# A decoder layer's paged attention: page loads in pairs with trailing rows and rope keys, and low parts moved between GpSimd and VectorE

## The chip, the cores and the metric

One core of one Trainium2 chip. The metric is the time of one execution on the device, in microseconds (us), as the median of several executions. A profiled execution has its own time and, inside it, the span from the first to the last instruction that the profiler recorded.

## The reference, cut to what matters

One decoder layer runs for 512 tokens of a new prompt and for 8 sequences of 8 new tokens each, which share all weights: a half-step of a SwiGLU feed-forward network, a combined projection, a convolution branch and an attention branch that are gated and merged, and a second half-step of a feed-forward network. The change touches only the attention of the 8 sequences over their cache:

```python
def one_seq(args):
    q_s, ckv_new, kpe_new, pages = args
    ckv = jnp.concatenate([cache_ckv_l[pages].reshape(past, KV_LORA), ckv_new], axis=0)
    kpe = jnp.concatenate([cache_kpe_l[pages].reshape(past, QK_ROPE), kpe_new], axis=0)
    k = build_keys(ckv, kpe, w_uk, k_head_norm)
    return attn_core(q_s, k, ckv, q_pos, k_pos, w_uv)
```

`past` is 2048 positions in 16 pages of 128. A page number comes from an int32 table and points into a pool. `build_keys` multiplies the 256 latent values of a position by `w_uk` (8 heads x 64), appends the 32 rope values and normalises each key by its root mean square; `attn_core` is 8 heads' softmax attention with the latents as values.

## The kernel before

**Precision.** Matmuls run on float32r operands split in two: `hi` is the rounded value (ScalarE copies it), `lo` the rest (a subtraction), and a product is hi x hi + hi x lo + lo x hi.

**The page stage.** `sequences` (L509) writes the loop over the 8 sequences: sequence 0 in straight code, then 1 to 4 in a hardware loop of two iterations of two, then 5, 6, 7 in straight code, on each compute engine. SyncE has a loop of its own (L778): sequences 0 and 1 are straight code, 2 to 7 a loop of three iterations of two. A sequence is 16 pages in 8 pairs. Three copies of a page are fetched, each by one transfer: transposed (`c_ring`, 128 KB, L731), as rows with the rope values beside them (`c_nat`, 144 KB, L737), and the rope keys transposed (`kpeT`, L742).
- *ScalarE* (`act_seq`, L1334): `pages_hi` (L1295) copies a pair of the ring into `cT_hi` (two slots); it needs the pair's transfers and TensorE done with the pair two before. For each page it copies scores from PSUM and squares the keys. In the same pass it makes `p_two` and the exponentials of the sequence before (`soft_act`) and the high parts of its rows (`pair_high`, L1328).
- *VectorE* (`dve_seq`, L2603): `pages_lo` (L2463) makes `cT_lo` of the next pair, 8 a sequence; the key sums (L2646); the softmax steps of the sequence before (`soft_dve`, L2497), the first of which (L2504) waits for GpSimd's squares; some taps of the convolution.
- *GpSimd* (`squares`, L950): for the sequence before, `split_pair` (L933), the low parts of row pairs 0 to 3, then `probabilities_low` (L941) in two halves, then row pairs 4 to 7; at the end it waits for this sequence's rows and squares their rope values (L962 to L964), for the key norms.
- *TensorE* (`pe_seq`, L1828): per page 12 products of 288 columns (L1861) that need `cT_lo` of the pair; after pages 3, 7, 11 and 15 one product with the rope keys of four pages (`kpe_scores`, L1818); at pages 12 and 15 the probabilities x values of the sequence before (L1781, L1782), each pair after `split_made`.

For sequence 7, the last, the sequence before (6) has its values multiplied without the split.

**The order of SyncE's queue.** SyncE issues everything in program order. `page_of` (L725) reads a page number from the table in SBUF into a register; it costs four instructions on the queue. `load_pages` (L744) goes by groups of four pages: four page numbers, a wait for the ring (`ct_lo`, both pairs two groups earlier), four ring transfers, a wait for `pe_scored`, four rope-key transfers with the same four registers, a wait for `pages_used`, four row transfers with the same registers. The ring has 8 slots (4 pairs), `kpeT` two groups, `c_nat` two sequences. L756 to L775 are the loads of sequence 0, woven into the waits of the stage before. Behind the loop come the first weights of the merge (`load_merge`, L611), which ScalarE splits in the midst of sequence 7 (L1367).

## Time and profile before

| | us |
|---|---|
| median of 3 runs | 1537.03 (1536.82 to 1539.36) |
| profiled execution, its own time | 1533.52 |
| its span, first to last instruction | 1531.5 |
| TensorE busy in the span | 1491.3 (97%) |
| VectorE / ScalarE / GpSimd busy | 1067.9 / 655.5 / 454.3 |
| page stage, first to last page product of TensorE | 706.8 to 1017.2 |
| `cT_lo` on VectorE | 64 of 0.69 (median) |
| `c_lo` on GpSimd | 48 of 1.20 (median) |

Busy times come from the profile's first part and from its groups of instructions; the start of an instruction is counted from the span's start. The profile doesn't count register, branch, semaphore and transfer-issuing instructions as busy, so SyncE has no busy time in it; its work is seen in the chain of waits (as "SPq") and in its timeline. TensorE's matmuls are pipelined and their ends are modelled, so its busy share is not its share of the peak. A busy time of 97% says little of a stage's limit: what counts is which wait ended last.

### The profile page before, as it was taken

Reading aid. Unit: us, or ns where it says so; the run is one execution under the profiler, and the core shown is the slowest. Engines: PE = TensorE matmul, PEld = TensorE weight load, DVE = VectorE, ACT = ScalarE, POOL = GpSimd, SP = SyncE. Lnnn points to the kernel's source line nnn. Section 1 sums busy time; section 2 is a strip of 40 time slices with the busy share of each in tenths; the row PEclk is TensorE's granted clock in tenths of the full one; section 3 lists DMA queues with packets and bytes.
Section 4 is the critical chain, followed back from the end, with each engine's and each line's share of the span. In section 5 each row is a group of like instructions: output and inputs, shape, how many; then the busy total and the mean of one; then the engine's idle time right before and its main releaser. Section 6 shows DMA issues by size and latency. Waiting matters only on the chain.

```text
span 1531.5 us, 31143 instructions
## 1 busy us (share of the span) xinstructions
PE 1491.3 (97%) x10771; PEld 1434.9 (94%) x10771; DVE 1067.9 (70%) x1738; ACT 655.5 (43%) x1215; POOL 454.3 (30%) x463
## 2 busy tenths in 40 slices
PE   8999999999999999999999888999999999999999
PEld 8999999999999999588888888888999999999999
DVE  7999898421269975865888788854759998985000
ACT  6444445322221242464666666642434444445111
POOL 4000002454465744320344333223551000005432
PEclk9999999999999999999999999999999999999999
DMA  6233234222333651003444443432222332332322
GB/s 176 70 103 103 82 97 116 78 83 75 82 83 100 83 116 47 13 4 99 129 127 129 124 125 111 128 106 72 83 83 56 109 97 85 106 92 81 91 77 82
DMA packets 245460, 141.69 MB, mean 93 GB/s; under 512 B 22705, under 2 KB 242290, under 8 KB 245362
## 3 DMA queue, kind: packets, MB, share of 16 engines
q1 hardware_dynamic: 244498, 139.97, 33.1%
q8 instruction: 54, 0.88, 0.2%
q10 hardware_dynamic: 864, 0.48, 0.1%
q14 instruction: 44, 0.36, 0.1%
HBM read 136.82 MB, written 3.58 MB: 92 GB/s over the span
## 4 chain that ended last, share of the span: by engine, by line
PE 52%; issue 24%; SPq 11%; POOL 7%; DVE 3%; ACT 1%; DMA 1%; POOLq 0%; DVEq 0%; ACTq 0%
PE ps L493 28%; PE ps L1522 14%; POOL w_lobuf L468 7%; SPq L726 3%; SPq L731 3%; SPq L742 3%; SPq L737 2%; PE ps L1861 2%; PE ps L1647 1%; PE ps L1701 1%; PE ps L1676 1%; PE ps L479 1%; PE ps L1691 1%; DMA w_rawbuf<-in_ffn_w_gu 1%; DVE cT_lo L2466 1%
## 5 line engine op out<-in xcount | busy, mean ns | idle before, releaser
L468 POOL TENSOR_TENSOR w_lobuf<-w_rawbuf,w_hibuf 128x256 fp32r<-128x256 f32 (+1 forms) x328 | 316.4, 996 | 801.4 <-ACT w_hibuf L461 801.3
L1522 PE MATMUL ps<-xs,w 128*128 128x288 f32 x3192 | 427.7, 296 | 0.8 <-DVE w L1984 0.8
L1522 PEld LDWEIGHTS ps<-xs,w 128*128 128x128 f32 x3192 | 426.8, 188 | 1.5 <-issue 1.5
L461 ACT ACTIVATE w_hibuf<-w_rawbuf 128x1024 fp32r<-128x1024 f32 (+1 forms) x89 | 104.4, 1173 | 353.3 <-PE ps L493 332.9
L2192 DVE SCALAR_TENSOR_TENSOR xT<-ps,xT 128x576 f32<-128x576 f32 x23 | 17.4, 756 | 202.4 <-PE ps L493 202.4
L1984 DVE TENSOR_TENSOR w<-w_raw,w 128x512 fp32r<-128x512 f32 x228 | 154.0, 690 | 0.3 <-ACT w L1029 0.2
L493 PE MATMUL ps<-a_hi,w_lobuf 128*128 128x288 f32 x682 | 147.5, 297 | 0.0
L493 PE MATMUL ps<-a_hi,w_hibuf 128*128 128x288 f32 x682 | 147.2, 296 | 0.0
L493 PE MATMUL ps<-x_hi,w_hibuf 128*128 128x288 f32 x656 | 142.2, 298 | 4.1 <-POOL w_lobuf L468 2.9
L493 PE MATMUL ps<-a_lo,w_hibuf 128*128 128x288 f32 x682 | 145.5, 294 | 0.0
L493 PE MATMUL ps<-x_lo,w_hibuf 128*128 128x288 f32 x656 | 140.8, 296 | 0.0
L493 PE MATMUL ps<-x_hi,w_lobuf 128*128 128x288 f32 x656 | 140.7, 296 | 0.0
L1029 ACT ACTIVATE w<-w_raw 128x512 fp32r<-128x512 f32 x228 | 132.2, 624 | 5.7 <-DVE w_raw L1978 2.4
L1861 PE MATMUL ps<-kq_hi,cT_hi 128*128 128x288 f32 x512 | 119.6, 316 | 14.7 <-DVE cT_lo L2466 9.3
L2215 DVE SCALAR_TENSOR_TENSOR y<-ext,cols,y 128x512 f32<-128x512 f32 x120 | 110.6, 922 | 4.1 <-DVE y L2215 1.4
L1861 PE MATMUL ps<-kq_hi,cT_lo 128*128 128x288 f32 x512 | 111.3, 299 | 0.0
L1861 PE MATMUL ps<-kq_lo,cT_hi 128*128 128x288 f32 x512 | 111.3, 299 | 0.0
L493 PEld LDWEIGHTS ps<-x_hi,w_hibuf 128*128 128x128 f32 x656 | 105.4, 188 | 5.8 <-POOL w_lobuf L468 4.1
L493 PEld LDWEIGHTS ps<-a_hi,w_hibuf 128*128 128x128 f32 x682 | 110.2, 189 | 0.0
L493 PEld LDWEIGHTS ps<-a_lo,w_hibuf 128*128 128x128 f32 x682 | 109.3, 188 | 0.0
L493 PEld LDWEIGHTS ps<-a_hi,w_lobuf 128*128 128x128 f32 x682 | 109.0, 188 | 0.0
L1861 PEld LDWEIGHTS ps<-kq_hi,cT_hi 128*128 128x128 f32 x512 | 84.1, 194 | 25.3 <-DVE cT_lo L2466 10.4
(335 smaller groups left out, 2602.6 us busy)
## 6 DMA issues: line engine op xcount, KB each, us to landing
w_raw<-in_ffn_w_gu SPq DMA_DIRECT2D x76, 256.0 KB, 2.9
up_rows<-in_ffn_w_gu SPq DMA_DIRECT2D x72, 256.0 KB, 3.2
c_nat<-in_pages_in SPq DMA_DIRECT2D x128, 144.0 KB, 2.2
c_ring<-in_pages_t SPq DMA_DIRECT2D x128, 128.0 KB, 2.1
w_rawbuf<-in_w_in SPq DMA_DIRECT2D x58, 256.0 KB, 3.2
w_rawbuf<-in_ffn_w_down SPq DMA_DIRECT2D x32, 384.0 KB, 4.0
w_rawbuf<-in_ffn_w_down SPq DMA_DIRECT2D x32, 320.0 KB, 3.4
w_rawbuf<-in_ffn_w_gu SPq DMA_DIRECT2D x24, 256.0 KB, 3.4
```

What stands on the lines that cost most here:

```text
L461: act.activation(w_hibuf[:, r % HIS, 0:size], w_rawbuf[:, r, 0:size], ACT.Copy).then_inc(w_hi_done, 1)
L468: ins = pool.tensor_tensor(w_lobuf[:, r, part], w_rawbuf[:, r, part], w_hibuf[:, r % HIS, part].bitcast(F32), ALU.subtract)
L493: mm = pe.matmul(ps[0:width, 2 * s + h, 0:HALF], a, b[:, k, h * HALF:(h + 1) * HALF], start=first and i == 0 and j == 0, stop=last and i = ...
L726: return sp.value_load(pages[0:1, ds(s * NP + t, 1)], min_val=0, max_val=pages_t.shape[0] - 1)
L731: sp.dma_start(c_ring[:, (4 * g + u + RING // 2) % RING, :], pages_t[ds(page, 1), :, :].rearrange("a p c -> (a p) c"))\
L737: sp.dma_start(c_nat[:, b, 4 * g + u, :], pages_in[ds(page, 1), :, :].rearrange("a p c -> (a p) c")).then_inc(nat_in[b][g], 16)
L742: sp.dma_start(kpeT[u * DR:(u + 1) * DR, g % 2, :], pages_k[ds(page, 1), :, :].rearrange("a d t -> (a d) t")).then_inc(kpe_in[g % 2], 16)
L1029: act.activation(w7[b][:, slot, 0, :], src, ACT.Copy).then_inc(w7_hi, 1)
L1522: mm = pe.matmul(ps[:, seven_bank(f, slot), 0:HALF], m, xs[:, slot, n, k, :], start=k == 0 and j == 0, stop=k == KH - 1 and j == 2)
L1861: mm = pe.matmul(ps[:, page_banks(t) + half, 0:KQ], a, m[:, half, cols], start=k == 0 and j == 0, stop=k == 1 and j == 2)
L1984: dve.tensor_tensor(w7[b][:, slot, 1, :], w7_raw[b][:, slot, 1, :], w7[b][:, slot, 0, :].bitcast(F32), ALU.subtract).then_inc(w7_lo, 1)
L2215: dve.scalar_tensor_tensor(dst, src, cw, dst, op0=ALU.mult, op1=ALU.add).then_inc(conv_p_step, 1)
```

## The change

- **The ring** is refilled pair by pair: each pair has its own semaphore and waits for the low part of the pair four before.
- **The rows trail**: row pairs 0 to 3 of a sequence are fetched with its ring pairs 4 to 7, row pairs 4 to 7 with the next sequence's ring pairs 0 to 3 (behind the loop for the last one). `nat_in` becomes one semaphore for a buffer, so who reads rows waits for all 16 pages.
- **The rope keys trail**: group 0 is fetched with ring pair 3, group 1 with 5, group 2 with 7, group 3 with pair 1 of the next sequence.
- **Page numbers** are read by `found` where each of the three is issued: two for a ring pair, two for a row pair, four for a group of rope keys.
- **Pages' low parts** (`pages_lo`) move from VectorE to GpSimd, but for sequence 0's. GpSimd does one a pair, with the row pairs' low parts at pairs 2, 3, 6 and 7; the low part of the next sequence's pair 0 comes ahead of the wait for the rows and the squares.
- **Probabilities' low parts** move from GpSimd to VectorE, at pair 5, with a semaphore `p_low` that TensorE waits for once a sequence.

```diff
--- before.py
+++ after.py
@@ -323,8 +323,8 @@
         prep_q, prep_tr, prep_copied, prep_mm, prep_lat, ready_new, uk_split = (sem(n) for n in (
             "prep_q", "prep_tr", "prep_copied", "prep_mm", "prep_lat", "ready_new", "uk_split"))
         ukT_done = sem("ukT_done")
-        nat_in = [[sem(f"nat_in{b}{g}") for g in range(NP // 4)] for b in range(2)]
-        ring_in = [sem(f"ring_in{g}") for g in range(2)]
+        nat_in = [sem(f"nat_in{b}") for b in range(2)]
+        ring_in = [sem(f"ring_in{j}") for j in range(RING // 2)]
         kpe_in = [sem(f"kpe_in{g}") for g in range(2)]
 
         def ring_pair(pp):
@@ -519,7 +519,7 @@
         PAIRS, EARLY_PAIRS = NP // 2, len(c_hi)
-        SPLITS = PAIRS + 2
+        SPLITS = PAIRS
@@ -533,7 +533,7 @@
 
         def pair_made(r, j):
 
-            return r * SPLITS + (EARLY_PAIRS + 1 if j < EARLY_PAIRS else j + 3)
+            return r * SPLITS + (j + 1)
 
         def high_made(r, j):
 
@@ -546,6 +546,12 @@
             return STACKED * HIGHS + (r - STACKED) * 2 + (1 + half)
 
         PEB = 6
+
+        def pages_lo(eng, s, pp):
+
+            eng.wait_ge(ct_hi, s * PAIRS + (pp + 1))
+            eng.tensor_tensor(cT_lo[:, pp % 2, :], ring_pair(pp), cT_hi[:, pp % 2, :].bitcast(F32), ALU.subtract).then_inc(ct_lo, 1)
+
 
         LN_MEAN, LN_VAR = (NS - 3, 8), (NS - 2, 10)
         THIRD = T // 3
@@ -725,59 +731,78 @@
             def page_of(s, t):
                 return sp.value_load(pages[0:1, ds(s * NP + t, 1)], min_val=0, max_val=pages_t.shape[0] - 1)
 
...
+            def found(s, t0, n):
+                return [page_of(s, t0 + u) for u in range(n)]
+
+            def load_ring(pp, two):
+
+                for u, page in enumerate(two):
+                    sp.dma_start(c_ring[:, (2 * pp + u + RING // 2) % RING, :], pages_t[ds(page, 1), :, :].rearrange("a p c -> (a p) c"))\
+                        .then_inc(ring_in[pp % (RING // 2)], 16)
+
+            def load_rows(b, pp, two):
+
+                for u, page in enumerate(two):
+                    sp.dma_start(c_nat[:, b, 2 * pp + u, :], pages_in[ds(page, 1), :, :].rearrange("a p c -> (a p) c")).then_inc(nat_in[b], 16)
+
+            def load_kpe(s, g):
+
+                four = found(s, 4 * g, 4)
+                if not (isinstance(s, int) and s == 0 and g < 2):
                     sp.wait_ge(pe_scored, s * (NP // 4) + (g - 1))
+                for u, page in enumerate(four):
+                    sp.dma_start(kpeT[u * DR:(u + 1) * DR, g % 2, :], pages_k[ds(page, 1), :, :].rearrange("a d t -> (a d) t"))\
+                        .then_inc(kpe_in[g % 2], 16)
+
+            def load_pair(s, b, pp, used=None):
+
+                two = found(s, 2 * pp, 2)
+                sp.wait_ge(ct_lo, s * PAIRS + (pp - 3))
+                load_ring(pp, two)
+                if pp >= PAIRS // 2:
+                    q = pp - PAIRS // 2
+                    two = found(s, 2 * q, 2)
                     if used is not None:
+                        sp.wait_ge(pages_used, used + (q + 1))
+                    load_rows(b, q, two)
+                elif used is not None:
+                    q = pp + PAIRS // 2
+                    two = found(s - 1, 2 * q, 2)
+                    sp.wait_ge(pages_used, used + (q + 1 - PAIRS))
+                    load_rows(1 - b, q, two)
+                if pp % 2:
+                    load_kpe(s - 1 if pp == 1 else s, 3 if pp == 1 else (pp - 3) // 2)
 
             sp.wait_ge(rows_done, 2 * NT + PT_TILES)
+            for pp in range(2):
+                load_ring(pp, found(0, 2 * pp, 2))
+            load_kpe(0, 0)
             sp.wait_ge(prep_q, 1)
+            for pp in range(6):
+                load_rows(0, pp, found(0, 2 * pp, 2))
             sp.wait_ge(prep_tr, 2)
             sp.wait_ge(uk_split, 1)
+            for pp in range(2, 4):
+                load_ring(pp, found(0, 2 * pp, 2))
+            load_kpe(0, 1)
+            for pp in range(6, PAIRS):
+                load_rows(0, pp, found(0, 2 * pp, 2))
+            for pp in range(4, PAIRS):
+                two = found(0, 2 * pp, 2)
+                sp.wait_ge(ct_lo, pp - 3)
+                load_ring(pp, two)
+            load_kpe(0, 2)
             sp.wait_ge(prep_mm, 2)
+            for pp in range(PAIRS):
+                load_pair(1, 1, pp)
             with sp.Fori(1, NS // 2) as i:
                 for b in range(2):
+                    for pp in range(PAIRS):
+                        load_pair(i * 2 + b, b, pp, i * (2 * PAIRS) + (EARLY_PAIRS + PAIRS * (b - 2)))
+            for q in range(PAIRS // 2, PAIRS):
+                sp.wait_ge(pages_used, EARLY_PAIRS + PAIRS * (NS - 3) + (q + 1))
+                load_rows(1, q, found(NS - 1, 2 * q, 2))
+            load_kpe(NS - 1, 3)
 
             sp.wait_ge(lat_mm, STACKED)
             for t in range(2):
@@ -938,28 +963,22 @@
                                    c_hi[j % EARLY_PAIRS][:, :, 0:KL].bitcast(F32), ALU.subtract)\
                     .then_inc(split_made, 1)
 
-            def probabilities_low(r, b, half):
-
-                t = slice(half * NP // 2, (half + 1) * NP // 2)
-                pool.wait_ge(p_done, exp_made(r, half))
-                ins = pool.tensor_tensor(p_two[:, t, 1, :], s_buf[:, b, t, :], p_two[:, t, 0, :].bitcast(F32), ALU.subtract)
-                if half:
-                    ins = pool.tensor_tensor(p_two[0:TS, NP, 1, :], s_buf[0:TS, b, NP, :], p_two[0:TS, NP, 0, :].bitcast(F32), ALU.subtract)
-                ins.then_inc(split_made, 1)
-
             def squares(s, b, uses, prev, nxt):
 
-                if prev and stacked(s):
-                    for j in range(EARLY_PAIRS):
-                        split_pair(s - 1, 1 - b, j)
-                    for half in range(2):
-                        probabilities_low(s - 1, 1 - b, half)
-                    for j in range(EARLY_PAIRS, PAIRS):
-                        split_pair(s - 1, 1 - b, j)
+                later = not (isinstance(s, int) and s == 0)
+                for pp in range(PAIRS):
+                    if later and pp < PAIRS - 1:
+                        pages_lo(pool, s, pp + 1)
+                    if prev and stacked(s):
+                        for j in ((), (), (0, 1), (2, 3), (), (), (4, 5), (6, 7))[pp]:
+                            split_pair(s - 1, 1 - b, j)
+                if not later:
+                    pool.wait_ge(ct_lo, PAIRS)
+                if nxt:
+                    pages_lo(pool, s, PAIRS)
                 if not nxt:
                     split_lo(pool, n_merge, n_merge % RAWS, KD * P)
-                for g in range(NP // 4):
-                    pool.wait_ge(nat_in[b][g], uses * 64)
+                pool.wait_ge(nat_in[b], uses * (16 * NP))
                 k = c_nat[:, b, :, KL:KL + DR]
                 pool.tensor_tensor(k, k, k, ALU.mult).then_inc(kpe_sq, 1)
 
@@ -1294,7 +1313,7 @@
 
             def pages_hi(s, pp):
 
-                act.wait_ge(ring_in[pp // 2 % 2], (s * 2 + (pp // 4 + 1)) * 64)
+                act.wait_ge(ring_in[pp % (RING // 2)], (s * 2 + (pp // 4 + 1)) * 32)
                 if not (isinstance(s, int) and s == 0 and pp < 2):
                     act.wait_ge(page_mm, s * NP + (2 * pp - 2))
                 act.activation(cT_hi[:, pp % 2, :], ring_pair(pp), ACT.Copy).then_inc(ct_hi, 1)
@@ -1327,7 +1346,7 @@
 
             def pair_high(r, b, j, uses):
 
-                act.wait_ge(nat_in[b][j // 2], uses * 64)
+                act.wait_ge(nat_in[b], uses * (16 * NP))
                 act.wait_ge(pages_used, r * PAIRS + (j + 1))
                 act.activation(c_hi[j % EARLY_PAIRS][:, :, 0:KL], c_nat[:, b, 2 * j:2 * j + 2, 0:KL], ACT.Copy).then_inc(p_done, 1)
 
@@ -1773,6 +1792,7 @@
                 pe.matmul(ps[:, 7, 0:HQ], ones[0:HQ, :], diag[:, :], start=True, stop=True).then_inc(max_mm, 1)
                 yield
                 if stacked(r + 1):
+                    pe.wait_ge(p_low, r + 1)
                     for j in range(PAIRS):
                         pe.wait_ge(split_made, pair_made(r, j))
                         for u in range(2):
@@ -2600,12 +2615,22 @@
 
                 tap(CT - 1, k, k + AT_LOOP if not isinstance(k, int) or k else None)
 
+            def probabilities_low(r, b):
+
+                for half in range(2):
+                    t = slice(half * NP // 2, (half + 1) * NP // 2)
+                    dve.wait_ge(p_done, exp_made(r, half))
+                    dve.tensor_tensor(p_two[:, t, 1, :], s_buf[:, b, t, :], p_two[:, t, 0, :].bitcast(F32), ALU.subtract)
+                dve.tensor_tensor(p_two[0:TS, NP, 1, :], s_buf[0:TS, b, NP, :], p_two[0:TS, NP, 0, :].bitcast(F32), ALU.subtract).then_inc(p_low, 1)
+
             def dve_seq(s, b, uses, prev, nxt):
                 soft = soft_dve(s - 1, 1 - b) if prev else None
                 taps = iter(range(PER))
                 for pp in range(NP // 2):
-                    if pp + 1 < NP // 2 or nxt:
-                        pages_lo(s, pp + 1)
+                    if isinstance(s, int) and s == 0 and pp + 1 < PAIRS:
+                        pages_lo(dve, s, pp + 1)
+                    if prev and stacked(s) and pp == 5:
+                        probabilities_low(s - 1, 1 - b)
                     if prev and pp < (5 if stacked(s) else 6):
                         next(soft)
                     if pp == 4 and nxt:
```

## Rows read from the trace of the kernel before

**Rows 1.** The page, part 4: the chain that ended last, by engine.
```profile
PE 52%; issue 24%; SPq 11%; POOL 7%; DVE 3%; ACT 1%; DMA 1%; POOLq 0%; DVEq 0%; ACTq 0%
```

**Rows 2.** The same chain from 768 to 996 us: shares by line; longest piece (start, us).
```profile
by line: issue 23.0%; SPq L726 15.4%; SPq L731 14.4%; SPq L737 14.0%; SPq L742 13.5%; DVE cT_lo L2466 2.9%; DVE page_ss L2646 2.4%; PE ps L1861 2.2%; DVE ln_acc L2579 1.0%; ACT cT_hi L1300 1.0%; DMA c_ring<-in_pages_t 0.9%; DVE mx L2520 0.9
...
839.74 2.65 issue
```

**Rows 3.** Timeline of SyncE in the loop: start us, us, engine, line, operation, count.
```profile
824.41 1.90 SPq L731 DMA_DIRECT2D c_ring<-in_pages_t  x4
826.56 1.84 SPq L742 DMA_DIRECT2D kpeT<-in_pages_k  x4
828.64 1.92 SPq L737 DMA_DIRECT2D c_nat<-in_pages_in  x4
833.41 1.89 SPq L731 DMA_DIRECT2D c_ring<-in_pages_t  x4
...
837.64 1.92 SPq L737 DMA_DIRECT2D c_nat<-in_pages_in  x4
845.27 0.87 SPq L731 DMA_DIRECT2D c_ring<-in_pages_t  x2
```

**Rows 4.** Timeline of SyncE in sequence 1 (straight code) and its last burst.
```profile
736.96 1.92 SPq L737 DMA_DIRECT2D c_nat<-in_pages_in  x4
741.29 1.88 SPq L731 DMA_DIRECT2D c_ring<-in_pages_t  x4
...
763.33 1.91 SPq L737 DMA_DIRECT2D c_nat<-in_pages_in  x4
```

**Rows 5.** Line 726, page numbers: duration ns min/median/max, first and last start us.
```profile
L726 SPq TENSOR_LOAD <-pages x140: 260/265/477, 644.7 to 988.0; - x140
```

**Rows 6.** SyncE's waits, 645 to 1020 us: total, times, longest.
```profile
SPq L737 <- DVE rope_rep L2441: 37.5, 1, 37.5
...
SPq L742 <- PE ps L1825: 3.0, 2, 2.5
```

**Rows 7.** Windows: us, busy PE, PEld, DVE, ACT, POOL (instructions), PEclk, DMA share, GB/s.
```profile
862.00:899.00 37.00, 33.73 (x244) 31.87 (x243) 32.81 (x53) 24.98 (x60) 15.07 (x12) 1.00 0.44 130
...
1007.00:1014.00 7.00, 6.44 (x30) 6.19 (x30) 5.27 (x9) 2.98 (x8) 3.31 (x4) 0.56 0.25 75
```

**Rows 8.** Line 1861's idle time by its end (us, times); ScalarE's waits, 744 to 1018.
```profile
  DVE cT_lo L2466: 19.7, 27
...
ACT cT_hi L1300 <- DMA c_ring<-in_pages_t: 13.3, 9, 3.5
```

**Rows 9.** Low parts by line (ns), and the timelines of VectorE and GpSimd where two meet.
```profile
L937 POOL TENSOR_TENSOR c_lo<-c_nat,c_hi x48: 1187/1200/1732, 747.2 to 966.0; 128x512 fp32r<-128x512 f32 x48
L2466 DVE TENSOR_TENSOR cT_lo<-c_ring,cT_hi x64: 627/692/1523, 706.0 to 1010.0; 128x512 fp32r<-128x512 f32 x64
L945 POOL TENSOR_TENSOR p_two<-s_buf,p_two x12: 1270/1279/1285, 760.8 to 957.9; 128x512 fp32r<-128x512 f32 x12
L947 POOL TENSOR_TENSOR p_two<-s_buf,p_two x6: 768/774/866, 763.9 to 959.1; 64x64 fp32r<-64x64 f32 x6
...
784.84 5.66 POOL L937 TENSOR_TENSOR c_lo<-c_nat,c_hi 128x512 fp32r<-128x512 f32 x4 [11.09 <-ACT c_hi L1332]
786.95 1.31 DVE L2466 TENSOR_TENSOR cT_lo<-c_ring,cT_hi 128x512 fp32r<-128x512 f32 x1
```

**Rows 10.** Timelines of SyncE, ScalarE and TensorE at the end of the stage.
```profile
992.96 2.69 SPq L737 DMA_DIRECT2D c_nat<-in_pages_in  x4
...
1001.21 1.06 ACT L461 ACTIVATE w_hibuf<-w_rawbuf 128x1024 fp32r<-128x1024 f32 x1 [6.06 <-DMA w_rawbuf<-in_w_conv_out]
1004.35 0.61 ACT L1300 ACTIVATE cT_hi<-c_ring 128x512 fp32r<-128x512 f32 x1
1007.56 0.37 PE L1808 MATMUL ps<-ones,den_sum 128*64 128x1 f32 x2 [3.11 <-DVE den_sum L2540]
1017.70 0.53 PE L493 MATMUL ps<-y_hi,w_hibuf 128*128 128x288 f32 x2
```

More of the change, by code:

```diff
@@ L726, in page_of @@
                 return sp.value_load(pages[0:1, ds(s * NP + t, 1)], min_val=0, max_val=pages_t.shape[0] - 1)
-            def load_ring(g, found):
-                for u, page in enumerate(found):
-                    sp.dma_start(c_ring[:, (4 * g + u + RING // 2) % RING, :], pages_t[ds(page, 1), :, :].rearrange("a p c -> (a p) c"))\
-                        .then_inc(ring_in[g % 2], 16)
-            def load_rows(b, g, found):
-                for u, page in enumerate(found):
-                    sp.dma_start(c_nat[:, b, 4 * g + u, :], pages_in[ds(page, 1), :, :].rearrange("a p c -> (a p) c")).then_inc(nat_in[b][g], 16)
@@ L739, in load_kpe @@
-            def load_kpe(g, found):
-                for u, page in enumerate(found):
-                    sp.dma_start(kpeT[u * DR:(u + 1) * DR, g % 2, :], pages_k[ds(page, 1), :, :].rearrange("a d t -> (a d) t")).then_inc(kpe_in[g % 2], 16)
-            def load_pages(s, b, used=None):
-                for g in range(NP // 4):
-                    found = [page_of(s, 4 * g + u) for u in range(4)]
-                    sp.wait_ge(ct_lo, s * PAIRS + (2 * g - 2))
-                    load_ring(g, found)
-                    sp.wait_ge(pe_scored, s * (NP // 4) + (g - 1))
-                    load_kpe(g, found)
-                    if used is not None:
-                        sp.wait_ge(pages_used, used + 2 * (g + 1))
-                    load_rows(b, g, found)
+            def found(s, t0, n):
+                return [page_of(s, t0 + u) for u in range(n)]
@@ L756, in _ @@
             sp.wait_ge(rows_done, 2 * NT + PT_TILES)
-            found = [page_of(0, u) for u in range(4)]
-            load_ring(0, found)
-            load_kpe(0, found)
+            for pp in range(2):
+                load_ring(pp, found(0, 2 * pp, 2))
+            load_kpe(0, 0)
             sp.wait_ge(prep_q, 1)
-            load_rows(0, 0, found)
-            for g in (1, 2):
-                load_rows(0, g, [page_of(0, 4 * g + u) for u in range(4)])
+            for pp in range(6):
+                load_rows(0, pp, found(0, 2 * pp, 2))
@@ L764, in _ @@
             sp.wait_ge(prep_tr, 2)
             sp.wait_ge(uk_split, 1)
-            found = [page_of(0, 4 + u) for u in range(4)]
-            load_ring(1, found)
-            load_kpe(1, found)
-            load_rows(0, 3, [page_of(0, 12 + u) for u in range(4)])
-            for g in (2, 3):
-                found = [page_of(0, 4 * g + u) for u in range(4)]
-                sp.wait_ge(ct_lo, 2 * g - 2)
-                load_ring(g, found)
-                sp.wait_ge(pe_scored, g - 1)
-                load_kpe(g, found)
+            for pp in range(2, 4):
+                load_ring(pp, found(0, 2 * pp, 2))
@@ L2461, in _ @@
             ins.then_inc(uk_split, 1)
-            def pages_lo(s, pp):
-                dve.wait_ge(ct_hi, s * PAIRS + (pp + 1))
-                dve.tensor_tensor(cT_lo[:, pp % 2, :], ring_pair(pp), cT_hi[:, pp % 2, :].bitcast(F32), ALU.subtract).then_inc(ct_lo, 1)
             dve.wait_ge(prep_tr, 3)
@@ L2483, in queries_lo @@
                 ins.then_inc(q_split, 1)
-            pages_lo(0, 0)
+            pages_lo(dve, 0, 0)
             dve.wait_ge(prep_lat, 2)
```

5 lines of the change are left out of this document (1 added, 4 removed).

## The prediction

> **What bounds the kernel now.** I began with the page's chain of what ended last [rows 1]: TensorE holds 52% of it, but SyncE's queue holds 11% and "issue" (time in which an engine waited for nothing that the profile shows) 24%. Work that only issues transfers has no place in the chain unless something waits for it, so the next view was the same chain cut to the loop over the cached pages, 768 to 996 us [rows 2]. There the four SyncE lines hold 15.4 + 14.4 + 14.0 + 13.5 = 57% and "issue" 23%; TensorE's page products (L1861) hold 2.2%. Its longest piece is 2.65 us of issue at 839.74: SyncE's branch back to the top of its loop. So in this stage the queue that fetches pages sets the pace.
>
> SyncE's own timeline says why [rows 3]. A group of four pages is three bursts: 4 transposed pages in 1.90 us, 4 rope keys in 1.84, 4 row pages in 1.92. A transfer starts every 0.52 us ((1.90 - 0.33)/3; the last one's issue is 0.33). From the end of the row burst (830.56) to the next ring transfer (833.41) lie 2.85 us, and in them are the four page-number loads of L726, which run one after another on the same queue. Less the 0.19 us that any transfer needs ahead of its issue (0.52 - 0.33), that is 0.66 us a load. In straight code the gap is 741.29 - 738.88 = 2.41 us, so 0.555 us a load [rows 4]. One loop sequence is then 48 x 0.52 + 16 x 0.66 = 35.5 us plus half of a back edge (the 839.56 to 845.27 gap is 5.7 us instead of 2.85), 37.0 us. The six loop sequences took 995.65 - 765.24 = 230.4 us [rows 4, 10], 38.4 us each.
>
> Does the queue ever rest? Between 645 and 1020 us it waited on semaphores among the sequences' page loads for 3.0 us (L742, twice); the 37.5 us at L737 lie before the sequences begin [rows 6]. There is no slack to put more into. TensorE, in contrast, has some: 33.7 us busy in a 37 us sequence [rows 7], and the waits that the change aims at are small: 19.7 us for the pages' low parts and 13.3 us of ScalarE for ring pages, over all eight sequences [rows 8].
>
> **The change part by part.**
>
> *Page-number loads.* Does a load happen once per page, or once per call? The trace of before has 140 of them [rows 5]. The code calls page_of 28 times for sequence 0 (twelve of these pages a second time), 16 for sequence 1 and 16 for each of six more: 140. So repeated ones are not shared. After the change the ring, the rows and the rope keys look up their pages separately: one load per page transfer. Transfers are three a page, 3 x 128 = 384, so loads are 384, 244 more. Where they fall:
> - Before the sequences: 20 instead of 12. These 8 are covered by the 37.5 us wait [rows 6]: nothing. Without it, they would cost 4.4 us.
> - Straight code from the second ring pair to the end of sequence 1, and behind the loop: 24 + 40 + 12 = 76 instead of 32, 44 more at 0.555 = 24.4 us.
> - The loop, six sequences: 48 instead of 16, 192 more at 0.66 = 126.7 us.
>
> *Waits.* A sequence has 20 places where SyncE checks a semaphore, instead of 12. In the loop each costs an address step of about 0.06 us: from the end of the ring burst to the key burst are 0.25 us (826.31 to 826.56), 0.19 of them the transfer's own. 48 x 0.06 = 2.9 us. The transfers are the same in number and size, so their issue costs nothing more.
>
> *What was slack.* The 3.0 us that SyncE waited before are swallowed: -3.0. The finer ring waits (pair p for the low part of pair p-4) are met well ahead when the queue paces everything: the low part it asks for needs only ScalarE's copy of a page pair that TensorE had two pairs earlier. That is also so across the trailing transfers. Group g's rope keys now come with ring pair 2g+3, so TensorE stops at pages 3, 7, 11 and 15 for them; but no ring wait needs TensorE further than that. The rows' last pairs come in the next sequence's first half, and GpSimd (L962) and VectorE (L2504) stand still for them; what they hold back is pair 1's low part, which SyncE asks for only four slots later (pair 5). I price these waits at nothing because the queue's 58 us a sequence cover them; if that cover were gone they would be the next thing (rival C).
>
> *Low parts on GpSimd.* 56 of the 64 move: 1.20 us there instead of 0.69 on VectorE (the 1.20 us is the same shape in L937) [rows 9], 56 x 0.51 = 29 us more of engine time, and nothing on the path. GpSimd's per-sequence load is 15.1 us [rows 7]; with eight lows instead of the probabilities' (2 x 1.28 + 0.77 us) it becomes about 21 of 58. The probabilities' low parts on VectorE replace lows of 8 x 0.69 us by about 2 us: it gains time that it doesn't need. Here a row bears on a risk: VectorE's low part at 786.95 took 1.31 us while GpSimd ran its own subtraction from 784.84 [rows 9]. More such overlaps could add up to 8 x 0.62 = 5 us a sequence to VectorE, which was busy 32.8 us of 37 [rows 7]; that too fits into 58. The Trainium skill, "SBUF — State Buffer", section "Who interferes with whom", has it that a VectorE instruction with two SBUF inputs contends with a GpSimd one that reads SBUF, and the loser blocks; by that rule the move speaks against itself, and the trace agrees (1.31 against 0.69 us).
>
> *Back edge and stalls.* A sequence grows from 220 to 356 instructions (four a load, three a transfer, one a wait). Of the 230.4 us of the six, 6 x 36.2 (with the waits' steps) + 5.7 for two back edges explain 223; 7 us are stretched issues. If they grow with the length they add 4 us, if not 0: I take 2.
>
> *The end of the stage.* From the last page transfer (995.65) to the first product of the merge (1017.70) are 22.0 us [rows 10]: the weight transfer right behind it, the ScalarE split that waits for it at 1001.21, then the high part of the next pair at 1004.35, then TensorE. That chain keeps its order, since the last rope keys are again issued just ahead of those weights. It becomes about 1.5 us longer (VectorE's sum of the probabilities now follows the page sums that ScalarE was late with). After it nothing changes.
>
> Sum: 24.4 + 126.7 + 2.9 - 3.0 + 2 + 1.5 = 154.5 us. The profiled execution took 1533.5 us (span 1531.5), 3.5 below the median of the runs, 1537.0. So 1688.0 against its own time, and 1691.5, say 1692, as a median.
>
> **The rivals.**
>
> *A, the forecast (0.84).* SyncE needs 48 x 0.52 + 48 x 0.66 + 20 x 0.06 = 57.8 us a sequence and everything else waits.
>
> *B, the stalls go and the loads are free (0.03), faster.* If a page-number load could run beside the transfers, the queue would again need 37 us, and the change would take away TensorE's 19.7 us for low parts and some of the ring waits: about 25 us, 1512. It turns at 25/236 = 0.1 us a load. Against it: the measured gaps of 2.85 and 2.41 us, in which nothing else is on the queue. The Trainium skill speaks for it, in "DMA: Bandwidth & Descriptors", section "Issuing engines are not separate DMA queues": the sequencer's time to initiate a DMA is usually small relative to the DMA. By that rule the queue isn't the bound; the trace disagrees, for the 48 issues of a sequence alone take 25 of its 37 us and leave the queue, with the loads, no rest.
>
> *C, loads at half price (0.04).* If only the load itself (0.265 us, [rows 5]) stayed and the register steps around it overlapped, 236 x 0.265 = 63 us; the queue then needs 39 us plus the new key and row waits of TensorE, GpSimd and VectorE: about 1600.
>
> *D, TensorE turns cold and becomes a second bound (0.09), slower still.* It now stands still four times a sequence for 4 to 8 us. After the 3.1 us wait ahead of 1007.56 [rows 10] the granted clock was 0.56 over 1007 to 1014 [rows 7]. At the lower level, 1.2 GHz, throughout, its 32 us of work would be 64, above 58: seven sequences x 6 = 42 us more, 1734. Against it: the rows show full clock again within the 7 us that follow, and four times 2 to 3 us fit into 58. It decides if the clock stays down for more than half of the work.
>
> **How the numbers follow.** Likeliest A, 1692. Its bounds: all loads at 0.555 us, 236 x 0.555 = 131 us instead of 151 and no stall growth give 1670; back edges that cost double (6 us), all stalls in proportion (2 more) and some cold TensorE time at the end of the stage (3) give 1704. Reaching towards D and for what I could not see of the instruction supply of a longer loop, the range is 1664 to 1722. About 0.2% is what a measurement of this kernel can tell from no change. Faster by more than that 0.03 (B), within it 0.01, slower 0.96.
>
> **What would show it.** In the changed kernel's profile: 384 loads at page_of; SyncE's sequences about 58 us long, with bursts of two transfers and 1.3 us between them; no wait of SyncE on ct_lo; in the loop's chain SyncE and "issue" above 85%; TensorE idle at the rope-key products and VectorE and GpSimd waiting for c_nat; TensorE below 60% busy between 780 and 1140 us, with a granted clock clearly below 1; the stage ending near 1174 instead of 1018; everything behind it shifted as a block. Wrong would be: fewer loads, a load below 0.4 us, or SyncE waiting on ct_lo or pe_scored for more than 10 us, which would put TensorE or the low parts in charge.

## The result and the profile after

The changed kernel takes 1666.74 us (median of 4 runs, 1665.25 to 1669.21) and the kernel before, in the same comparison, 1536.92 (1534.81 to 1539.36): a ratio of 1.0846 [1.0825, 1.0867], slower by 129.8 us. The forecast was 1692, in a range of 1664 to 1722. Direction, mechanism and range hold; the size was 25 us too large. In the profiled executions the span grew from 1531.5 to 1664.2 us, +132.7 where the sum had +154.5. One run of this document, an execution of E3 with 1794.27 us at a granted clock of 0.751, was in a slow state and is left out of E3's numbers below.

The page of the changed kernel: span, busy times, TensorE and its granted clock in 40 slices, and the chain by engine.

```profile
span 1664.2 us, 31938 instructions
PE 1530.0 (92%) x10771; PEld 1473.6 (89%) x10771; DVE 1048.8 (63%) x1700; ACT 657.0 (39%) x1215; POOL 505.5 (30%) x501
PE   8999999999999999997577776867999999999999
PEclk9999999999999999998887788878999999999999
PE 49%; issue 26%; SPq 14%; POOL 8%; DMA 1%; ACT 1%; DVE 1%; POOLq 0%; ACTq 0%
```

SyncE's queue now holds 14% of the chain, and "issue" 26%, against 11 and 24 [rows 1]. TensorE was at work nearly all the time except in slices 19 to 28, the stage with the cached pages; its clock falls in the same slices. The chain cut to that stage (780 to 1110 us), by line, with one of its longest pieces:

```profile
by line: SPq L732 32.8%; issue 30.3%; SPq L746 10.2%; SPq L740 10.1%; SPq L754 9.4%; POOL c_lo L962 2.2%; POOL cT_lo L553 1.9%; PE ps L1881 1.5%; PE ps L1801 0.6%; PE ps L1802 0.6%; DMA kpeT<-in_pages_k 0.6%; SPq L760 0.4%; PE ps L1845 0.4%
...
887.78 2.68 issue
```

The reading of page numbers, now L732, goes from 15.4% [rows 2] to 32.8%, while the three transfer lines fall from 14 or so to 10 each. With "issue" the four lines make up 92.8%. Not all of this "issue" is the queue's: up to 818 us the chain runs through GpSimd, with idle pieces of 13.32 us (at 787.25) and 5.55 (774.52). From 820 to 1110 us, where it runs through the queue, the same view reads

```profile
by line: SPq L732 37.2%; issue 24.0%; SPq L746 11.6%; SPq L740 11.2%; SPq L754 10.7%; PE ps L1881 1.7%; PE ps L1801 0.7%; PE ps L1802 0.7%; DMA kpeT<-in_pages_k 0.6%; SPq L760 0.4%; PE ps L1845 0.4%; SPq L766 0.2%; SPq L771 0.2%; SPq L752 0
```

which is 94.7% with its 24.0% of "issue". The count of the reads, over the whole kernel (duration ns min/median/max, first and last start us):

```profile
L732 SPq TENSOR_LOAD <-pages x384: 260/267/479, 645.1 to 1128.6; - x192
```

384 instead of 140 [rows 5], and one of them takes what it took. SyncE's timeline in the loop (start, us, engine, line, operation, count), to be laid beside [rows 3]:

```profile
857.78 1.84 SPq L754 DMA_DIRECT2D kpeT<-in_pages_k  x4
861.21 1.21 SPq L740 DMA_DIRECT2D c_ring<-in_pages_t  x2
863.82 0.87 SPq L746 DMA_DIRECT2D c_nat<-in_pages_in  x2
866.26 0.86 SPq L740 DMA_DIRECT2D c_ring<-in_pages_t  x2
868.49 0.86 SPq L746 DMA_DIRECT2D c_nat<-in_pages_in  x2
871.75 1.86 SPq L754 DMA_DIRECT2D kpeT<-in_pages_k  x4
875.18 0.90 SPq L740 DMA_DIRECT2D c_ring<-in_pages_t  x2
```

A burst of two takes 0.86 us, and 1.4 to 1.6 us pass before the next one (2.4 before the four keys): the queue spends more time on finding pages than on asking for them. SyncE's waits on semaphores, 645 to 1160 us (total, times, longest), and the waits of the others for rows, keys and low parts (longer ones, up to GpSimd's 185.8 us for ScalarE's copies, are of engines that wait for each other):

```profile
SPq L732 <- DVE rope_rep L2461: 35.7, 1, 35.7
SPq L811 <- POOL cT_lo L553: 10.8, 1, 10.8
SPq L776 <- PE ps L1677: 6.7, 1, 6.7
```
```profile
POOL c_nat L983 <- DMA c_nat<-in_pages_in: 82.2, 6, 15.8
PE ps L1845 <- DMA kpeT<-in_pages_k: 60.5, 20, 6.1
PE ps L1881 <- POOL cT_lo L553: 57.6, 8, 10.0
DVE kpe_ss L2520 <- POOL c_nat L983: 55.3, 6, 10.2
```

The first of these waits lies ahead of the sequences, as before [rows 6], and so does the one at L776 (`rows_done`); L811, and two of 5 us at the merge's weights (L624, L621), stand in the code behind the page loads. So none is at the page loads of the sequences. TensorE, GpSimd and VectorE stand still for the trailing keys and rows, as the prediction had it, and for low parts whose pages came late. They wait beside each other and all for the queue, so their sum means nothing.

### The profile page after: what moved, and what is told of

Read it like the earlier page. It is cut to its first block, busy times and chain, and to the rows that moved or that the text cites. A ratio compares the mean times of both kernels' runs of the same rounds, so it can differ in the third digit from the quotient of the medians.

```text
span 1664.2 us, 31938 instructions
## 1 busy us (share of the span) xinstructions
PE 1530.0 (92%) x10771; PEld 1473.6 (89%) x10771; DVE 1048.8 (63%) x1700; ACT 657.0 (39%) x1215; POOL 505.5 (30%) x501
## 4 chain that ended last, share of the span: by engine, by line
PE 49%; issue 26%; SPq 14%; POOL 8%; DMA 1%; ACT 1%; DVE 1%; POOLq 0%; ACTq 0%
PE ps L493 26%; PE ps L1541 13%; SPq L732 7%; POOL w_lobuf L468 6%; SPq L746 2%; PE ps L1881 2%; SPq L740 2%; SPq L754 2%; PE ps L1666 1%; PE ps L1720 1%; PE ps L1695 1%; POOL cT_lo L553 1%; PE ps L1822 1%; POOL c_lo L962 1%; DMA w_rawbuf<-in_ffn_w_gu 1%
## 5 line engine op out<-in xcount | busy, mean ns | idle before, releaser
L1881 PE MATMUL ps<-kq_hi,cT_hi 128*128 128x288 f32 x512 | 131.5, 341 | 59.4 <-POOL cT_lo L553 57.6
L1881 PEld LDWEIGHTS ps<-kq_hi,cT_hi 128*128 128x128 f32 x512 | 94.9, 216 | 66.4 <-POOL cT_lo L553 36.0
L2671 DVE TENSOR_REDUCE page_ss<-sq 128x8 f32<-128x512 f32 x128 | 84.2, 677 | 99.9 <-ACT sq L1370 99.8
L553 POOL TENSOR_TENSOR cT_lo<-c_ring,cT_hi 128x512 fp32r<-128x512 f32 x56 | 77.4, 1382 | 185.8 <-ACT cT_hi L1319 185.8
L1881 PE MATMUL ps<-kq_hi,cT_lo 128*128 128x288 f32 x512 | 120.2, 319 | 0.0
L1881 PE MATMUL ps<-kq_lo,cT_hi 128*128 128x288 f32 x512 | 118.7, 316 | 0.0
```

Of the source, the lines that this page charges most:

```text
L553: eng.tensor_tensor(cT_lo[:, pp % 2, :], ring_pair(pp), cT_hi[:, pp % 2, :].bitcast(F32), ALU.subtract).then_inc(ct_lo, 1)
L1881: mm = pe.matmul(ps[:, page_banks(t) + half, 0:KQ], a, m[:, half, cols], start=k == 0 and j == 0, stop=k == 1 and j == 2)
L2671: dve.tensor_reduce(page_ss[:, t, :], sq[:, u, 0:H * DN].rearrange("p (h d) -> p h d", d=DN), AX, ALU.add).then_inc(page_red, 1)
```

## The experiments

All ten kernels were timed against the kernel before, in three groups, each on one chip but every group on another; the medians of before in them were 1535.25 (E1 to E4), 1534.35 (E5 to E8) and 1535.9 us (E9, E10). Two theories stood at the start: the loss is the number of page-number reads (each holds SyncE's queue for about 0.55 us), or it is the trailing order and the new waits that starve TensorE.

### E1 and E10: the kernel before, with more reads and nothing else

```diff
                     load_kpe(g, found)
+                    found = [page_of(s, 4 * g + u) for u in range(4)]
                     if used is not None:
```

E10 has this line; E1 has it and the same one ahead of the wait for `pe_scored`. They apply to sequences 1 to 7: 112 and 224 reads more.

> The kernel before with one thing added: in sequences 1 to 7 SyncE reads the four page numbers of a group three times, ahead of the ring, of the rope keys and of the rows. 224 more loads, nothing else moved, no trailing transfers. The queue theory (SyncE's queue paces the page stage and a load runs alone on it): in the changed kernel a load without its own address step takes 0.56 us, so 224 x 0.56 = 125 us less the 3 us of slack, 1659 us (1650 to 1672), nearly all of the change's own loss. Rival (the loss comes from the waits that the trailing rows and rope keys put on TensorE, GpSimd and VectorE): the loads are mostly hidden, below 1560.

> The kernel before with the page numbers of each group read twice in sequences 1 to 7 (112 more loads, half of e1). If the queue is the bound throughout, the price a load is the same as in e1, 0.55 us: 112 x 0.55 = 62 us less at most 3 us of slack, 1595 us (1590 to 1600). Rival (the first loads are partly hidden, a knee between): below 1585.

Measured: E1 1659.29 us, ratio 1.0801 [1.0779, 1.0823], +124.0. E10 1594.65, ratio 1.039 [1.0375, 1.0404], +58.8. The reads in E1 and the chain from 768 to 1100 us:

```profile
L726 SPq TENSOR_LOAD <-pages x364: 260/267/479, 645.7 to 1115.8; - x182
```
```profile
by line: SPq L726 37.6%; issue 25.1%; SPq L737 12.4%; SPq L731 11.5%; SPq L742 10.8%; DMA c_ring<-in_pages_t 0.6%; PE ps L1783 0.5%; PE ps L1784 0.4%; DVE cT_lo L2468 0.2%; SPq L748 0.2%; SPq L755 0.2%; ACT cT_hi L1302 0.2%; SPq L751 0.2%; 
```

E1 costs 124.0 / 224 = 0.554 us a read and E10 58.8 / 112 = 0.525; with the 3.0 us of slack that both swallow, 0.567 and 0.552. The second 112 reads cost 65.2 us, the first 58.8, and of this difference of 6.4 us the slack makes 3.0, and the rest is within the two intervals (3.4 us either way for E1, 2.2 for E10): so the price is linear as far as these runs can tell, and there is next to no slack to be filled first. E1 keeps the order, the waits and the engines of before, and loses nearly all that the change loses: reads alone suffice.

### E2: the change, without its additional reads

```diff
-                four = found(s, 4 * g, 4)
+                four = found(s, 4 * g, 4) if four is None else four
...
                 two = found(s, 2 * pp, 2)
+                four, last[0] = (last[0] or []) + two, two
...
                     q = pp - PAIRS // 2
-                    two = found(s, 2 * q, 2)
...
                     q = pp + PAIRS // 2
-                    two = found(s - 1, 2 * q, 2)
```

The trailing rows and keys take the ring pairs' page numbers that are at hand. It leaves out that those transfers fetch the right pages; their number, size, places and waits are those of the change. 168 reads are left.

> The changed kernel with the page numbers of the ring pair used again for the row pair and the rope keys that are issued beside it, in sequences 1 to 7: 216 loads fewer, every transfer of the same size at the same place of the queue, every wait kept. It leaves out fetching the right pages for the trailing rows and rope keys. Queue theory: 216 x 0.57 = 123 us come back, 1544 us (1535 to 1556). Rival (trailing waits): it stays above 1620.

Measured: 1549.24 us, ratio 1.0085 [1.0064, 1.0106], +14.0. Trailing order, pairwise waits and moved low parts are all there, and 116 us of the loss are gone, 0.54 for each of the 216 reads. What is left is near 20 reads x 0.55 + 48 waits x 0.06 = 13.9 us (28 reads more than before, 8 of them under the wait ahead of the sequences). The rival theory falls.

### E3 and E4: pairs without trailing; the low parts alone

```diff
             def load_pair(s, b, pp, used=None):
                 two = found(s, 2 * pp, 2)
                 sp.wait_ge(ct_lo, s * PAIRS + (pp - 3))
                 load_ring(pp, two)
-                if pp >= PAIRS // 2:
...
+                if pp % 2:
+                    load_kpe(s, pp // 2, last[0] + two)
+                last[0] = two
+                if used is not None:
+                    sp.wait_ge(pages_used, used + (pp + 1))
+                load_rows(b, pp, two)
```

E3 (against the changed kernel, above) refills pair by pair and moves the low parts, but rows and keys follow their own ring pairs and share the numbers: 160 reads. E4 has SyncE's code of before, and of the change only GpSimd's `pages_lo` and VectorE's `probabilities_low`.

> The changed kernel with rows and rope keys no longer trailing in sequences 1 to 7: per pair two page numbers, the ring pair, at odd pairs four rope keys, then the row pair, all with the same page numbers. 16 loads a sequence as before, but refilled by pairs, with the low parts moved as in the change. Queue theory: the queue is as long as before but for 8 more waits a sequence (0.06 us each, 3 us in all), so 1535 us (1526 to 1545); the difference to e2 is what the trailing itself costs or brings. Rival (fine ring waits and the moved low parts bring the speed that was meant): below 1520.

> The kernel before with only the low parts moved: pages' low parts on GpSimd, probabilities' low parts on VectorE, SyncE's queue untouched. Queue theory: the queue covers it, 1537 us (1530 to 1543). Rival (GpSimd's 1.2 to 1.4 us a low part, and its meeting VectorE's two-input subtractions, are on the path): 56 x 0.5 = 28 us more, about 1560.

Measured: E3 1544.34 us, 1.0058 [1.0038, 1.0078], +9.1, where 12 x 0.55 + 2.9 is 9.5: the 1535 us expected (1526 to 1545) had left out 12 more reads in sequence 0's loads. The speed that was meant did not come. E4 1537.55, 1.0004 [0.999, 1.0017], no difference. SyncE's only wait at the page loads of sequences 1 to 7 in E4, and what TensorE waited for most at its page products, 705 to 1030 us:

```profile
SPq L748 <- PE ps L1827: 2.1, 1, 2.1
```
```profile
PE ps L1863 <- POOL cT_lo L553: 14.0, 10, 2.7
```

Moving the low parts to an engine that takes twice as long for one costs nothing and brings nothing here. That the queue decides when the pages come would be the reason, and E8 below, where they cost 3.4 us, fits it.

### E5 to E8: one instruction for several page numbers

Reads at 0.55 us on a full queue suggest the opposite edit: fewer of them. One load can fill several registers.

```diff
+            def many(s, t0, n):
+                return list(nc.values_load_multi_w_load_instructions(pages[0:1, ds(s * NP + t0, n)], engines=[mybir.EngineType.SP],
+                                                                     min_val=0, max_val=pages_t.shape[0] - 1,
+                                                                     skip_runtime_bounds_check_because="page numbers come from the table")[1])
...
-                    found = [page_of(s, 4 * g + u) for u in range(4)]
+                    found = many(s, 4 * g, 4)
```

It also leaves out the range check of each number. E5 is the kernel before with it, E8 is E4 with it, E6 is E3 with one for each pair, and E7 is the whole change with it in `load_pair` and `load_kpe`.

> The kernel before with one edit: in sequences 1 to 7 the four page numbers of a group come by one load instruction that fills four registers, without the range check of each number. The queue shrinks from 37 us a sequence to about 25.0 + 4 x 0.4 + 1 = 28 us. Queue theory: the queue really is the bound of the kernel before, so it gets faster until the next bound, TensorE's 32.5 us of work and its 4 us of waits a sequence: 37 instead of 38.4 us in the loop and 5 us in sequence 1, so about 1522 us (1512 to 1531). Rival (the queue was only just not in the way, TensorE's own chain sets the pace before): 1535 us, no change.

> e3 (pairs, not trailing, low parts moved) with one load instruction for the two page numbers of a pair: the queue is 25 + 8 x 0.4 + 1.2 = 29.5 us. If the fine ring waits and the moved low parts are worth anything, it shows here, where the queue is out of the way: 8 to 12 us below e5, about 1512. If they are worth nothing, equal to e5; if GpSimd's 1.2 us a low part is now on the path, 5 to 15 us above it.

> The whole change, trailing rows and rope keys too, right pages everywhere, with one load instruction wherever page numbers are read in sequences 1 to 7 (20 a sequence instead of 48). The queue is 25 + 20 x 0.42 + 1.2 = 34.6 us a sequence. Queue theory: all of the change's loss goes: 1525 to 1540. Rival (trailing waits): with the queue out of the way the waits for the trailing rows and keys remain, above 1560.

> e4 (the kernel before with the low parts moved) with e5's single loads. Against e5 it tells what the moved low parts are worth when the queue covers nothing: theory of the change, VectorE's lateness (19.7 us of TensorE's waits) goes, 10 us below e5; rival (GpSimd slower and in program order with the row pairs' low parts), 5 to 15 us above e5.

| kernel | median us | ratio to before [95%] |
|---|---|---|
| E5, before | 1526.49 | 0.9945 [0.9929, 0.9961] |
| E8, low parts moved | 1529.88 | 0.9971 [0.9959, 0.9982] |
| E6, and pair by pair | 1531.13 | 0.9975 [0.9966, 0.9985] |
| E7, and trailing (the change) | 1541.38 | 1.0043 [1.0027, 1.0058] |

In E5 the loads, SyncE's timeline, its waits from 705 to 1030 us, and the chain from 768 to 990:

```profile
L729 SPq TENSOR_LOAD <-pages x28: 295/299/317, 733.2 to 983.0; - x28
```
```profile
826.52 1.92 SPq L742 DMA_DIRECT2D c_nat<-in_pages_in  x4
829.14 1.88 SPq L736 DMA_DIRECT2D c_ring<-in_pages_t  x4
```
```profile
SPq L747 <- PE ps L1830: 60.2, 21, 7.2
```
```profile
by line: issue 20.9%; DVE page_ss L2651 12.8%; PE ps L1866 12.1%; DVE cT_lo L2471 11.9%; DVE mx L2525 3.6%; ACT sq L1356 3.4%; ACT cT_hi L1305 3.1%; DVE s_buf L2520 2.8%; DVE y L2220 2.6%; ACT s_buf L1327 2.6%; DVE s_buf L2659 2.0%; ACT p_t
```

The gap between rows and ring is 829.14 - 828.44 = 0.70 us instead of 2.85 [rows 3], and in sequence 1 it is 0.52 instead of 2.41 [rows 4]. 24 groups x 2.15 and 4 x 1.89, 59 us, are freed on the queue, and only 7.9 reach the end: SyncE now waits 60.2 us for the page scores at L747, and no SyncE line is left among the lines that the chain shows. The bound has passed to the engines. E5 beats both kernels and is the best version found; its gain is within the expected range but smaller than its value, since TensorE and VectorE were closer behind the queue than I had thought.

The ladder below it prices the change's other parts where the queue is no longer full. The low parts on GpSimd cost 1529.88 - 1526.49 = 3.4 us, with intervals that just touch. Pair by pair adds 1.2, which is nothing that these runs can tell, and it holds more on the queue: 12 plain reads in sequence 0 and eight loads a sequence of two numbers instead of four loads of four. Neither theory's value came: E8 was to be 10 us below E5 or 5 to 15 above, E6 8 to 12 below, equal, or 5 to 15 above, and it is 4.6 above. Trailing adds 10.2, but with it the queue gets more reads, and E7 ends just above the 1525 to 1540 that were expected. In E7 the loads are (whole kernel), with the chain from 768 to 990 us:

```profile
L735 SPq TENSOR_LOAD <-pages x140: 303/473/488, 650.6 to 1004.3; - x140
```
```profile
by line: issue 26.5%; SPq L735 20.7%; SPq L759 14.9%; SPq L745 14.9%; SPq L751 14.8%; PE ps L1886 3.0%; POOL cT_lo L553 1.9%; POOL c_lo L967 1.8%; SPq L765 0.6%; POOL c_nat L988 0.5%; SPq L776 0.3%; SPq L771 0.3%; SPq L757 0.2%; PE ps L1850
```

With 20 loads a sequence, most at 0.47 us, the queue is still the bound. So E7 doesn't tell what trailing is worth by itself. The loads of E6, all of two numbers, say which of them take 0.47:

```profile
L735 SPq TENSOR_LOAD <-pages x56: 462/476/497, 736.6 to 988.0; - x56
```

A load of two numbers takes 0.47 us here, in E9 and in E7 (108 of its 140, the other 32 being of four), and one of four 0.30 in E5, E8 and E7. The expectations had 0.4 for both.

### E9: trailing with a short queue

E9 is E2 with `many(s, 2 * pp, 2)` for the ring pairs: 8 loads a sequence and the change's order of transfers. Like E2 it leaves out that the trailing transfers fetch the right pages.

> e2 (the change with the ring pair's page numbers used again for the trailing rows and rope keys; the right pages of those are left out) with one load instruction a pair: 8 in a sequence, the same queue as e6, 29.5 us. The only difference to e6 is that rows and rope keys trail. If trailing costs nothing of its own: within 3 us of e6 once the 12 page numbers and transfers behind the loop are counted (12 x 1.07 = 13 us of queue ahead of the merge's weights, of which the short queue should cover a part), 1531 to 1540. Rival (trailing has its own price: GpSimd and VectorE wait for the last rows, TensorE for the keys): 1545 or more.

Measured: 1537.81 us, ratio 1.0012 [1.0, 1.0024]. By the ratios that is 0.0037 x 1535 = 5.7 us above E6, give or take 2.4 by the two intervals (E6 ran on another chip, so the times themselves aren't compared), and inside the expected 1531 to 1540. The longest wait of SyncE at page loads, in E9 first and then in E6, and the end of SyncE's page loads in the same order:

```profile
SPq L745 <- POOL cT_lo L553: 39.8, 28, 2.9
```
```profile
SPq L751 <- PE ps L1799: 16.4, 5, 4.6
```
```profile
984.69 1.85 SPq L759 DMA_DIRECT2D kpeT<-in_pages_k  x4
988.40 7.91 SPq L751 DMA_DIRECT2D c_nat<-in_pages_in  x8
998.73 1.85 SPq L759 DMA_DIRECT2D kpeT<-in_pages_k  x4
1000.68 0.41 SPq L624 DMA_DIRECT2D w_rawbuf<-in_w_conv_out  x1
```
```profile
994.63 0.40 SPq L624 DMA_DIRECT2D w_rawbuf<-in_w_conv_out  x1
```

In E9 the queue rests: it waits 39.8 us for the low parts that free its ring. Its page loads in the loop end at 986.54, but 12 reads and 12 transfers stand behind the loop, ahead of the merge's weights, which go out at 1000.68 instead of 994.63. These 6.05 us, of one execution each, agree with the 5.7: with a queue that has room, what trailing costs is accounted for by its tail. Even there it gains nothing over E6.

## Why the prediction was right, and where it was off

**What bounds the kernel**, right. The queue read off the gap of 2.85 us was the bound; E1 and E10 show it, without any other edit. It was so by less than the prediction made of it, and one reading of [rows 2] was wrong: the chain's longest piece from 768 to 996 us was not the 2.65 us at 839.74, but

```profile
917.24 3.06 issue
...
933.69 3.18 PE ps L1861 x24
```

From 925 to 972 us that chain runs through the transfers, ScalarE, VectorE and TensorE, so these were close behind the queue, as E5's gain of only 7.9 us shows too. The Trainium skill, "DMA: Bandwidth & Descriptors", section "Issuing engines are not separate DMA queues", says that the sequencer's time to initiate a DMA is usually small relative to the DMA. By the profile an issue took 0.52 us [rows 3] and a page's transfer 2.1 to 2.2 from issue to landing, so each one is the smaller part; but the issues run one after another. The runs disagree with the rule for this stage: what stands on the issuing queue set the time in E1, E10 and the change.

**244 more reads, 8 of them covered**, right: 384 in the trace, and no cost of the eight shows. But only four of them lie ahead of the 37.5 us wait; the other four were covered by one of 3.3 us in before (L765, for VectorE's `kq_lo`), which the prediction didn't name. The next ring burst started at 705.10 us instead of 705.76.

**0.66 us a read in the loop**, the step that failed: "The loop, six sequences: 48 instead of 16, 192 more at 0.66 = 126.7 us." The timeline above has it by kind of burst, each gap less the 0.19 us that a transfer needs ahead of its issue and the 0.06 of a wait's step. Ring pair, rows at 864.69 to ring at 866.26: (1.57 - 0.25)/2 = 0.66. Rows, ring at 867.12 to rows at 868.49: (1.37 - 0.25)/2 = 0.56. Keys, 869.35 to 871.75: (2.40 - 0.25)/4 = 0.54. The register steps of L726 before and L732 after, within the loop, go with it:

```profile
L726 SPq FUSED_REGOPS  x182: 46/152/164, 774.7 to 988.3; - x182
L726 SPq TENSOR_LOAD <-pages x92: 262/265/287, 774.8 to 988.0; - x92
```
```profile
L732 SPq FUSED_REGOPS  x402: 46/152/160, 777.1 to 1115.7; - x134
L732 SPq TENSOR_LOAD <-pages x286: 262/267/291, 777.2 to 1115.4; - x143
```

Before, two register steps a read: the check of about 0.15 us, and one of about 0.05. Now 1.4. That the short one is the address, and is shared by reads whose address is at hand, is an inference from the counts. The measured part is the price: most of the added reads are of the cheap kind. 192 x 0.55 is 105.6 instead of 126.7 us, 21 less, and that is nearly the whole error of 22. The lower price was in the range as a bound (1670), by the straight code's row; I took the price of the loop's own row, which held reads of the dearer kind alone. With it the law is short: 236 x 0.55 = 130 us, measured 129.8. That this comes out to the last digit is luck: waits and slack cancel, and so nearly do the two terms that follow.

**Waits 2.9, slack -3.0**, right as far as E2, E3 and E10 can tell.

**Back edges and stalls 2 us**, too small. The last page transfer ended at 995.65 before [rows 10] and at 1131.16 now, +135.5. The corrected terms give 24.4 + 105.6 + 2.9 - 3.0 = 129.9, so 5.6 are left for back edges and stretched issues, 4.6 of them in the loop; had the stalls grown in proportion it would have been 4. What they consist of wasn't resolved. The loop's body didn't grow as counted: by the trace SyncE ran some 216 and then 326 instructions a sequence, not 220 and 356, since an added read needs one register step and not two.

**End of the stage +1.5**, wrong in sign. From the last page transfer to the merge's first product it was 22.05 us and is now 1149.13 - 1131.16 = 17.97:

```profile
1129.32 1.84 SPq L754 DMA_DIRECT2D kpeT<-in_pages_k  x4
```
```profile
1134.87 1.06 ACT L461 ACTIVATE w_hibuf<-w_rawbuf 128x1024 fp32r<-128x1024 f32 x1 [21.66 <-DMA w_rawbuf<-in_w_conv_out]
...
1138.01 0.61 ACT L1319 ACTIVATE cT_hi<-c_ring 128x512 fp32r<-128x512 f32 x1
```
```profile
1129.55 0.28 PE L1828 MATMUL ps<-ones,den_sum 128*64 128x1 f32 x2
1149.13 0.53 PE L493 MATMUL ps<-y_hi,w_hibuf 128*128 128x288 f32 x2
```

ScalarE's split starts 3.71 us behind the last page transfer instead of 5.56 [rows 10]. TensorE's sum of the probabilities (L1828) starts at 1129.55, while everything waits for the queue; in before it came at 1007.56, behind that split and a wait of 3.11 us [rows 10]. I had argued only with the order of that chain, not with what the engines finish while they stand still. 135.5 - 4.1 and 1.3 us behind the stage make the 132.7 of the span.

**Work priced at nothing** stayed covered, as predicted: no page load of SyncE waits at L740, L746 or L754. The cover was the long queue. E5, E8 and E9 show what comes out without it: 3.4 us for the low parts, 6 for the tail, and SyncE waiting for TensorE or the low parts. The low parts on GpSimd took (ns min/median/max)

```profile
L553 POOL TENSOR_TENSOR cT_lo<-c_ring,cT_hi x56: 1257/1286/2342, 739.2 to 1142.9; 128x512 fp32r<-128x512 f32 x56
L553 DVE TENSOR_TENSOR cT_lo<-c_ring,cT_hi x8: 675/682/774, 707.7 to 735.9; 128x512 fp32r<-128x512 f32 x8
```

1.29 us instead of the 1.20 taken from another line [rows 9], and up to 2.34. One of these beside VectorE:

```profile
805.36 2.33 POOL L553 TENSOR_TENSOR cT_lo<-c_ring,cT_hi 128x512 fp32r<-128x512 f32 x1 [2.48 <-ACT cT_hi L1319]
```
```profile
805.32 1.21 DVE L2530 TENSOR_TENSOR s_buf<-s_buf,k_inv 128x1024 f32<-128x1024 f32 x1
```

The Trainium skill, "SBUF — State Buffer", section "Who interferes with whom", has a VectorE instruction with two SBUF inputs contend with a GpSimd one that reads SBUF, and one of them block; this pair agrees with it (the 2.33 us are 1.04 more than the usual 1.29, and VectorE's instruction ran beside it for 1.17), and E4 shows that it had no price here.

**The rivals.** B (free reads, 1512) and C (half price, 1600) fall: a read costs 0.55 us in E1. D's first half happened, its second not. TensorE's windows (us, busy PE, PEld, DVE, ACT, POOL, PEclk, DMA share, GB/s):

```profile
892.00:948.00 56.00, 38.83 (x234) 37.19 (x232) 26.95 (x44) 24.43 (x58) 21.89 (x17) 0.80 0.30 85
...
780.00:1140.00 360.00, 248.75 (x1491) 232.55 (x1489) 174.62 (x272) 152.95 (x359) 126.27 (x98) 0.83 0.30 85
```

The granted clock was 0.83 over the stage: part of it at the 1.2 GHz level after TensorE's pauses (behind its wait of 10.00 us ahead of 1140 us it was 0.50 from 1140.2 to 1143.5, and 1.00 again from 1144.2 to 1149). But busy time stayed at 38.83 of 56 us, and the queue never waited for it, so it bounded nothing. It did make one sign wrong: "below 60% busy" came out as 248.75/360 = 69%, since work at the lower level takes longer (the product of `kq_hi` and `cT_lo` took 319 ns in the mean, against 299 in before). The sequence time of the signs, about 58 us, was 343.5/6 = 57.3 (774.46 to 1117.98). That is luck: 57.8 had the reads 3.5 us a sequence too dear, and had left out back edges and stretched issues, about 3.0. The stage ended at 1149 and not near 1174.

## What to carry to other kernels

Before an edit that issues transfers in smaller groups, count what each group does on the issuing queue besides the transfers (address steps, reads of indices, range checks, waits) and see on its timeline whether it rests; on a queue that is full in the gaps too, each added instruction is paid in full. Take the price from a gap of the same kind as the one that is added, since a read that is repeated may need fewer steps than the first one of its kind. And when a queue is the bound, read several indices with one instruction before reordering anything: that, with the range check left out, is what paid here, 7.9 us, while the finer and later order brought nothing that these runs show, even with the queue relieved.

## What the runs showed of the hardware

- A dynamic page number costs SyncE's queue 0.54 to 0.66 us: 0.27 for the load, the rest, as read here, register steps of the range check and address. One load that fills four registers took 0.30 us without the check (E5). How much of the saving is the single load and how much the missing check was not tried apart.
- A load of two page numbers into two registers took longer, 0.47 us (E6, E9, 108 of E7's 140), than one of four into four, 0.30 (E5, E8, the other 32 of E7). Why is open.
- SyncE's branch back to the top of its loop cost one piece of 2.68 us of the chain (887.78) after the change and 2.65 before (839.74), though by the trace its body of two sequences grew from some 430 to some 650 instructions. The other one of before took 3.06 (917.24).
- The 128x512 subtraction on GpSimd took 1.29 us, 1.9 times VectorE's 0.68.
